# Moving the last 128 channels of branch B's 31-tap convolution from TensorE to ScalarE and GpSimd

## The reference, cut to what matters

```
glu    = b_in[..., :1024] * sigmoid(b_in[..., 1024:])
conv_b = causal depthwise convolution of glu, 31 taps, per channel
y_b    = silu(layernorm(conv_b + bias)) * silu(b_z)
```

## Time and profile before

| | us |
|---|---|
| three runs | 4301.25, 4305.78, 4576.11 (median 4305.78) |
| the profiled execution's own time | 4298.67 |
| its span on the slowest core (core 6) | 4297.1 |
| spans of the eight cores | 4275.0 to 4297.1 |
| granted TensorE clock, mean of a core | 0.992 to 0.995 |
| busy time of PE, DVE, ACT, POOL on core 6 | 4139.4, 2320.9, 1578.3, 211.9 |

### The profile page before, as it was taken

How to read it: one execution, slowest core, us unless ns; L and a number is a source line. 1 busy time by engine, 2 the same in 40 slices (tenths; PEclk the granted TensorE clock), 3 DMA queues, 4 the chain that set the end, 5 groups by cost and what they waited for, 6 DMA issues and landing times.

```text
span 4297.1 us, 72177 instructions; the slowest of 8 cores (4275.0 to 4297.1 us)
## 1 busy us (share of the span) xinstructions
PE 4139.4 (96%) x24601; PEld 1941.1 (45%) x25036; DVE 2320.9 (54%) x3637; ACT 1578.3 (37%) x2586; POOL 211.9 (5%) x560
## 2 busy tenths in 40 slices
PE   7999999989989999999999999999999999999998
PEld 3444444444434444444444444444444444444443
DVE  3574444644367543774457743576437754377534
ACT  3254232262423622336252451325333362233622
POOL 0100000100000000100001000010001000010000
PEclk9999999999999999999999999999999999999999
DMA  9885678865777312452254422453235521345212
GB/s 164 155 175 139 159 202 187 177 140 139 179 212 181 123 69 88 154 150 95 77 176 136 138 75 79 144 148 112 79 113 183 137 107 69 124 135 161 76 69 94
DMA packets 186373, 571.56 MB, mean 133 GB/s; under 512 B 34224, under 2 KB 100256, under 8 KB 142496
## 3 DMA queue, kind: packets, MB, share of 16 engines
q1 hardware_dynamic: 151280, 377.40, 29.8%
q0 software_dynamic: 23712, 113.75, 13.5%
q10 hardware_dynamic: 11024, 75.76, 4.8%
HBM read 518.72 MB, written 128.05 MB: 151 GB/s over the span
## 4 chain that ended last, share of the span: by engine, by line
PE 85%; DVE 5%; issue 4%; DMA 3%; ACT 3%; SPq 0%; DVEq 0%; ACTq 0%; POOL 0%; POOLq 0%
PE ps L619 56%; PE ps L591 15%; PE ps L851 4%; PE ps L1260 4%; PE ps L1079 4%; ACT tmp_t L252 1%; DVE tmp_t L258 1%; ACT ya L252 1%; PE ps L683 1%; DVE tmp_t L255 1%; DVE co L255 1%; PE ps L1145 1%; DMA tmp_t<-x 1%; DVE co L735 1%; DVE tT L255 0%
## 5 line engine op out<-in xcount | busy, mean ns | idle before, releaser
L619 PE MATMUL ps<-hT,wring 128*128 128x512 bf16 x8837 | 2018.3, 380 | 46.1 <-DVE tmp_t L255 18.5
L619 PEld LDWEIGHTS ps<-hT,wring 128*128 128x128 bf16 x9088 | 877.7, 98 | 1088.6 <-issue 62.3
L255 DVE TENSOR_TENSOR tmp_t<-ps,tmp_t 128x512 f32<-128x512 f32 (+1 forms) x756 | 480.0, 637 | 991.5 <-PE ps L619 844.4
L252 ACT ACTIVATE tmp_t<-ps 128x512 f32<-128x512 f32 (+3 forms) x966 | 549.1, 584 | 893.6 <-PE ps L619 509.6
L591 PE MATMUL ps<-hT,wring 128*128 128x512 bf16 x3113 | 719.6, 382 | 21.0 <-ACT tmp_t L252 11.6
L252 ACT ACTIVATE tmp_t<-ps,pc 128x512 f32<-128x512 f32 (+1 forms) x432 | 277.0, 645 | 971.7 <-PE ps L619 916.5
L591 PEld LDWEIGHTS ps<-hT,wring 128*128 128x128 bf16 x3200 | 305.4, 98 | 359.7 <-issue 25.2
L252 ACT ACTIVATE tmp_t<-co 128x512 bf16<-128x512 f32 x256 | 157.4, 627 | 477.2 <-DVE co L262 464.8
L255 DVE TENSOR_TENSOR tmp_t<-tmp_t 128x512 f32<-128x512 f32 (+2 forms) x292 | 188.5, 645 | 184.7 <-ACT tmp_t L252 168.2
L735 DVE SCALAR_TENSOR_TENSOR co<-smp,co 128x512 f32<-128x512 bf16 x360 | 269.5, 748 | 24.1 <-DVE co L735 0.5
L252 ACT ACT_TABLE_LOAD x153 | 196.3, 1283 | 133.8 <-PE ps L591 31.5
(11 more groups left out here) (110 smaller groups left out, 2492.9 us busy)
## 6 DMA issues: line engine op xcount, KB each, us to landing
wring<-wbf SPq DMA_DIRECT2D x196, 1024.0 KB, 5.8
wring<-wblk POOLq DMA_DIRECT2D x76, 1024.0 KB, 13.2
wbf<-wring ACTq DMA_DIRECT2D x68, 1024.0 KB, 6.7
wring<-glp SPq DMA_DIRECT2D x258, 135.0 KB, 4.5
wring<-cwd SPq DMA_DIRECT2D x116, 256.0 KB, 5.4
tmp_t<-xp SPq DMA_DIRECT2D x56, 512.0 KB, 6.6
tmp_t<-x SPq DMA_DIRECT2D x32, 512.0 KB, 5.5
yp<-tmp_t POOLq DMA_DIRECT2D x24, 512.0 KB, 4.1
```

The source lines that it names most:

```text
L252: S.op("act", lambda e: e.activation(out=out, in_=in_, func=func, **kw), reads=reads, writes=writes)
L255: S.op(eng, lambda e: e.tensor_tensor(out=out, in0=in0, in1=in1, op=op), reads=reads, writes=writes)
L619: ins = e.matmul(outs[i], lhsT=wk(sl[i], kk, jj * 128), rhs=rr[i][:, kk, 0:NT], start=(kk == 0), stop=(kk == 7))
```

## The change

Passes 2 to 7 take chunk 7 of either tile off TensorE too (`P.ew` gets (0, 7) and (1, 7)). For chunk 7 ACT makes each tap's product: tap 0 with the bias straight into `co`, taps 1 to 30 into one of two f32 buffers `pr`; POOL adds each product to `co` in place with a tensor_tensor of 128x512 f32. The 62 items of a pass wait in a list of their own, `ew_adds`: one is emitted after each glu unit and two after each unit of `stage_a`. The buffers `xe` are three in place of two, the weights move to another place in `smp` and are two small DMAs, and `smp` is free for them only when the sample segment's `co` and `v` are. A method `finish` is added to `Sched`, and nothing calls it.

```
+                P.ew = ((0, 0), (1, 0), (0, 7), (1, 7)) if pr > 0 else ()
 def ew_weights():
     for n, j in enumerate(ew_j):
+        o = 820 + n * DEPTH * KB
+        DMA(smp[:, o:o + DEPTH * KB], cwe[j], (), ("xw",) + HR(SS) + RA(SS, "ya") + RA(SS, "yb")
+            + sum((CO(SS, c) for c in range(NCH)), ()) + (R(SS, "v"),), "xw", eng="pool")
 def ew_start(P, T, j):
+    i = P.ew.index((T, j)) % 3
     ...
+    if j == 7:
+        def prod(k):
+            pr = smp[:, 948 + k % 2 * TS_:948 + k % 2 * TS_ + TS_]
+            ACT(pr, xe[:, k:k + TS_], AF.Copy, rx, (("xp", k % 2),), scale=ew_w(l, j, k))
+            TT(acc, acc, pr, ALU.add, ra + (("xp", k % 2),), ra, eng="pool")
+        ew_adds.append(((T, j), lambda: ACT(acc, xe[:, 0:TS_], AF.Identity, rx + ("pc",), ra, scale=ew_w(l, j, 0),
+                                            bias=pcol(l, j, R_CBB))))
+        for k in range(1, KB):
+            ew_adds.append(((T, j), lambda k=k: prod(k)))
+        return
+ew_adds = []
+def ew_add(n):
+    for _ in range(min(n, len(ew_adds))):
+        ew_adds.pop(0)[1]()
 def ew_flush(key):
     while any(k == key for k, _ in ew_taps):
         ew_pop(1)
+    while any(k == key for k, _ in ew_adds):
+        ew_add(1)
 # stage_glu, after each unit
     ew_pop(3)
+    ew_add(1)
 # stage_a, after each ac/ax unit
     step()
+    ew_add(2)
 # stage_a, after each az/ab unit
     step()
     ew_pop(2)
+    ew_add(2)
```

More of the change, by code:

```diff
@@ L125, in barrier, with finish @@
                 self.streams[e].append((waits, None, None))
+    def finish(self):
+        waits = [(e, self.count[e]) for e in self.ENG if self.count[e] > 0]
+        waits += [(("dma", lane), 16 * n) for lane, n in self.lane_n.items()]
+        kn = self.known["sp"]
+        self.streams["sp"].append(([(k, v) for k, v in waits if kn.get(k, 0) < v], None, None))
     def bank(self):
@@ L405, in build_program @@
                 P.pend = {}
-                P.ew = ((0, 0), (1, 0)) if pr > 0 else ()
+                P.ew = ((0, 0), (1, 0), (0, 7), (1, 7)) if pr > 0 else ()
                 P.sq = "sp" if pr == 0 or len(passes) == 2 else "pool"
@@ L706, in ew_w @@
         def ew_w(l, j, k):
-            o = 600 + ew_j.index(j) * DEPTH * KB + l * KB + k
+            o = 820 + ew_j.index(j) * DEPTH * KB + l * KB + k
             return smp[:, o:o + 1]
@@ L711, in ew_weights @@
             for n, j in enumerate(ew_j):
-                o = 600 + n * DEPTH * KB
-                DMA(smp[:, o:o + DEPTH * KB], cwe[j], (), ("xw",) + HR(SS) + RA(SS, "ya") + RA(SS, "yb"), "xw", eng="pool")
+                o = 820 + n * DEPTH * KB
+                DMA(smp[:, o:o + DEPTH * KB], cwe[j], (), ("xw",) + HR(SS) + RA(SS, "ya") + RA(SS, "yb") + sum((CO(SS, c) for c in range(NCH)), ()) + (R(SS, "v"),), "xw", eng="pool")
         def ew_start(P, T, j):
@@ L717, in ew_start @@
             q, ti = P.tile[seg.k]
-            i = P.ew.index((T, j)) % 2
+            i = P.ew.index((T, j)) % 3
             xe = smp[:, 272 * i:272 * i + 272].bitcast(BF16)
```

## The result

The changed kernel takes 1.080 times as long as the kernel before (95% interval 1.077 to 1.083). Its profiled execution takes 4651.6 us against 4298.7, and 4649.6 us of span against 4297.1, so 353 us more; the forecast was 205 us more, and its range ended at 4600.

What follows compares the result with a forecast made beforehand. It took PE (TensorE) as the bound, with DVE nearly as loaded where the adds go: 4298.7 - 21.8 (matmuls removed) + 222 (37 us a pass, six passes) + 5 (weights load) = 4504 us, range 4280 to 4600.

Steps and rivals of the forecast that it cites:

- The step: Glu and stage A: POOL's SBUF-reading adds hold DVE's two-input instructions too, at the full 1.15 us per add.
- Rival 1: Ac/ax units: DVE is never held by adds, only POOL waits; 4282 us, chance 0.27.
- Rival 2: POOL's add is cheap, 0.54 us; 4334 us, chance 0.1.
- rival 3: POOL's add is dear, 2.17 us, and ACT also stands behind POOL; about 4900 us, chance 0.1.
- the line 14.3 - 8.7 = 5.6: Glu, per pass: DVE delayed 14.3 us, PSUM banks hide 8.7, PE stalls 5.6.
- the 8.7 us: Glu: slack from four pairs of PSUM banks, letting DVE fall further behind PE without stalling it.
- the 20 to 50 us a pass: Passes 2 to 7: the forecast case's range of added time, giving 4402 to 4582 us; late queued adds got no further price.
- its 5.1 us: Glu: ACT waits for its first input behind unit 7, making unit 8's DVE multiply 5.1 us late.
- +16.7 and +11.2 a half: Stage A, first and second half: time added per pass, with 1.8 us for removed chunks carried in each.
- 5.2 - 1.8: First az/ab eight of stage A: 5.2 us lost per pass to 15 adds, less 1.8 for the removed chunk.
- the 4.4 us of free time: First ac/ax eight of stage A: DVE's free time, subtracted from 18.4 us of adds, leaving 13.3 lost with one PSUM move.
- 5 us for a second weights load: Pass 2, once: the xe load queues behind two weight loads on one lane, adding 5 us to the path.

Runs made afterwards that it cites:

- adds against writes: Changed kernel, two POOL memsets replacing each add: 4451.7 us; same swap with late start, xe loads on SP and halo copies on DVE: 4342.4 against 4560.2 us with adds.
- The single runs: Changed kernel with chunk 7's items started late: 4622.9 us; that plus its xe loads on SP's queue: 4605.1; changed kernel with halo copies on DVE: 4606.2.
- first item only: Changed kernel without taps 1 to 30 of chunk 7; tap 0 on ACT and its xe load stay: 4347.5 us, ratio 1.010.
- the last experiment: Kernel before the change, with tap weights loaded in pass 1 into the idle gfin buffer: 4302.9 us against 4298.7.
- the taps on DVE: Changed kernel with chunk 7's 31 taps on DVE instead of ACT and POOL, list emptied at the old pace: 4545.8 us, ratio 1.056.

## Why the prediction was right or wrong

**The kind was right.** Slower, because an add that reads SBUF and a DVE instruction with two SBUF inputs hold each other up, both ways. The step rested on one direction; the other is shown by the 3.38 us pair, and by adds against writes: with reads 1209 and 1006 ns, without 752 and 751. Rival 1 (never held, 4282) is out. The rule of the Trainium skill (SBUF — State Buffer, section Who interferes with whom) says that these two contend, whichever comes first, and that a GpSimd instruction that only writes doesn't contend with a VectorE instruction of two SBUF inputs; the traces agree, at 752 ns beside 379 us of POOL writes. Where it says that the other fully blocks, the trace has a little less: 0.55 us behind the add for an instruction of 0.75. Rival 2 (4334) and rival 3 (about 4900) fall with the add's length.

**What the port itself cost** was not undervalued. DVE's rows grew by 228 us for 360 adds, 0.63 us each averaged, where I charged up to 1.15; the ac/ax unit came out at 4.92 us for 5.2. An instruction of line 265 that meets an add is 0.89 us longer in the mean, not 1.28, since it issues a little behind the add and part of it runs beside it; and many adds fell into waits. In all the port is worth 200 to 218 us.

**The add** takes 1254 ns at the least and 1276 in the middle, not 1090. The row I scaled it from, a one-input instruction over 1024 elements, was too cheap by 15%. GPSIMD Engine Reference of the Trainium skill, section Performance versus the Vector engine, gives 1124 by proportion, an estimate, and the measurement decides: 1276. In the same sum that would be 7.6 us more a pass; but with the longer add the ac/ax unit still came out below the forecast, so this is not what the sum lacked.

**The failed step is the line 14.3 - 8.7 = 5.6: the delay of DVE in glu that the banks were to absorb for good.** The banks did absorb it, and more: DVE fell back by 14.8 us further, and PE lost 3.8 us in glu. But PE had to give that time back in stage A. There the banks are not the only tie between DVE and PE: `finish` needs DVE's result of one unit before, and there PE stood 7.43 us in every pass. For DVE the 8.7 us were to come back behind stage A, and 1.2 did. That is 7.5 us a pass. Three terms of the sum were too small beside it: DVE's own delay in glu, 18.6 for 14.3, and the two halves of stage A, 22.3 for 16.7 and 18.5 for 11.2. Together the four are 24.7 us a pass, 148 in six, which is the gap between 4504 and 4652. That the wait in front of `finish` is what took the 8.7 us back is read from the trace and the order of the code; no run moved it.

**Glu** counted ACT's wait and eight adds for DVE, and was 4.3 us short. The trace shows two things it left out. ACT, POOL and the DMA are tied together: the add stands behind an xe load that waits for a glp write, the product behind the add's buffer, the sigmoids behind the product (6.12, 7.79 us). And the last such load stands in front of the halo copy (5.28 us of DVE). I had listed these queues and given them no price "beyond the 20 to 50 us a pass". The single runs give them one: ACT's first wait and what comes with it 71 us (first item only, with the 21.8 us of matmuls added), where the sum has nothing for it once the slack has covered its 5.1 us; and of the queue effects 29, 18 and 45 us could be mended.

**Stage A** was forecast at +16.7 and +11.2 a half and came out, for DVE, at +22.3 and +18.5. In pass 3 the first ac/ax eight went from 31.3 to 48.3 us, +17.0 for 13.3; the az/ab eight from 35.3 to 39.6, +4.3 for 5.2 - 1.8. By DVE's starts the price of an add was not the error there: 18.4 us of adds less 0.7 for the saved move is 17.7. The error is the 4.4 us of free time that I let them use. It was DVE waiting for ACT behind a convolution, and the adds wait for the same ACT then: the two units with a convolution grew by 3.1 us each (8.82 for 5.75, 10.12 for 7.05), and DVE's wait from 2.74 to 5.80 us. In the second half, too, I credited DVE's free time and got 13 where 18.5 + 1.8 = 20.3 was lost of 24.2 us of adds.

**Once, in pass 2:** 5 us for a second weights load. PE's wait there went from 9.2 to 12.8 us in the mean of the eight cores (9.62 to 11.36 on the two profiled here), so the load cost about 3.5. But the wait of the earlier trace rows was the glp write's, as the last experiment shows: the step read the releaser of the last wait as the cause of the whole, and its size came out near by luck.

**The products** cost nothing, as forecast (4347.6 with, 4347.5 without). The matmuls removed, 21.8 us, show in single halves of stage A: with the first item only the second half is 2.1 us shorter for PE than before, and with the taps on DVE the first half is 1.7 shorter (67.1 us for 68.9), so twelve chunks are some 23 us. No run removed the chunks alone.

The sum, all against 4298.7: -22 matmuls, +71 what ew_start brings (4347.5), 0 products, +104 POOL's queue (4451.7), +200 the port (4651.6). PE's time at the lower clock and its wait in front of `finish` are inside these terms.

## What to carry to other kernels

An idle GpSimd is not free time when VectorE runs two-input instructions in the same stretch: weigh its SBUF reads as VectorE time (an instruction that met an add was 0.89 us longer here), and compare it with letting VectorE do the work itself (0.79 us for a whole tap, with no queue of POOL behind it). Slack in buffers lends time to a late engine only as far as the next place where the other needs its result: look for that place before you count the slack as a gain. Work put into an in-order queue is priced by what stands behind it, not by its engine's idle share: small copies and DMA issues in POOL's queue cost as much here as half the port. Spread deferred work evenly; blocks of 25 and 21 taps in a pass cost 70 to 85 us more than the same taps spread.

## What the runs showed of the hardware

A GpSimd add of 128x512 f32, both inputs in SBUF, takes 1.25 to 1.28 us alone and up to 1.72 where it waits for DVE. A GpSimd memset of the same tile takes 0.53 us and leaves DVE's two-input instructions at 0.75. A VectorE scalar_tensor_tensor is recorded up to 2.31 us long when an add holds it; its wait is inside its row, so it looks like slow work and not like idle time.
